# Expert products' scratch laid out by token tile and second half-key, two expert blocks stored at once

## What is computed

```
def _peer(x, wq, keys, u_tab, v_tab):
    ...
    s = jnp.einsum('thcd,hcnd->thcn', q, keys)
    v1, i1 = lax.top_k(s[:, :, 0], PEER_TOPK)
    v2, i2 = lax.top_k(s[:, :, 1], PEER_TOPK)
    ...
    cidx = (i1[..., :, None] * N_KEYS + i2[..., None, :])...
    top_s, pos = lax.top_k(cand, PEER_TOPK)
    ...
        a = jnp.einsum('td,tkd->tk', xt, u_tab[it])
        hid = (gelu(a) * gt)
        return jnp.einsum('tk,tkd->td', hid, v_tab[it])
```

## Time and profile before

| | us |
|---|---|
| median of 3 runs | 3742.63 (3737.31 to 3744.31) |
| the profiled execution, its own time | 3735.37 |
| its span | 3733.6 |
| PE busy | 2471.0 (66%) |
| DVE busy | 2762.9 (74%) |
| POOL busy | 1246.5 (33%) |
| ACT busy | 332.7 (9%) |

### The profile page before, as it was taken

The page is one execution under the profiler, slowest core; times in us unless marked ns, Lnnn a source line. Parts: engine busy times, 40 slices in busy tenths (PEclk is TensorE's granted clock), DMA queues, the critical chain, the costliest instruction groups (busy, mean ns, idle before and its releaser), DMA issues.

```text
span 3733.6 us, 30440 instructions
## 1 busy us (share of the span) xinstructions
PE 2471.0 (66%) x11208; PEld 1892.2 (51%) x11208; DVE 2762.9 (74%) x3210; ACT 332.7 (9%) x832; POOL 1246.5 (33%) x1273
## 2 busy tenths in 40 slices
PE   7798799978975777959988999999978000000000
PEld 7687689545743444535677877777767000000000
DVE  5331220979989997787789889976655999988888
ACT  1212311000002221000100000000000000000000
POOL 2420000122233332223222223232222577777772
PEclk9899899988986657989999999999999555555555
DMA  8774355898998999989999999999998999999998
GB/s 245 219 232 121 143 190 179 292 397 332 341 405 343 406 419 375 422 343 414 421 422 423 423 423 423 423 421 424 423 382 336 413 407 410 409 390 370 392 373 348
DMA packets 297908, 1332.43 MB, mean 357 GB/s; under 512 B 70752, under 2 KB 136832, under 8 KB 146336
## 3 DMA queue, kind: packets, MB, share of 16 engines
q0 software_dynamic: 138624, 945.22, 62.9%
q1 hardware_dynamic: 126400, 371.83, 26.7%
q10 hardware_dynamic: 32736, 13.44, 1.4%
HBM read 1282.60 MB, written 57.20 MB: 359 GB/s over the span
## 4 chain that ended last, share of the span: by engine, by line
PE 35%; DMA 27%; DVE 22%; POOL 8%; issue 6%; another core or an unknown queue 1%; ACT 1%; ACTq 1%; SPq 0%; DVEq 0%; POOLq 0%
PE low L1559 18%; DMA arena<-in_ut 16%; PE low L1900 10%; DVE arena L1375 7%; DVE acc L1391 5%; DMA arena<-in_peer_v,arena 5%; POOL arena L611 4%; POOL arena L620 4%; DMA arena<-in_w 2%; DMA arena<-in_peer_u,arena 2%; PE low L1633 1%; PE acc L1633 1%; DMA arena<-y_scratch_b 1%; DVE low L1391 1%
## 5 line engine op out<-in xcount | busy, mean ns | idle before, releaser
L1391 DVE SCALAR_TENSOR_TENSOR acc<-arena,acc 128x2048 f32<-128x2048 f32 x443 | 1042.6, 2354 | 262.4 <-DMA arena<-in_peer_v,arena 226.7
L1559 PE MATMUL low<-arena 128*128 128x192 f32 (+1 forms) x4096 | 1064.8, 420 | 100.6 <-DMA arena<-in_w 77.3
L1900 PE MATMUL low<-arena 128*128 128x256 f32 x4096 | 915.5, 383 | 110.1 <-DMA arena<-in_ut 109.0
L1559 PEld LDWEIGHTS low<-arena 128*128 128x128 f32 x4096 | 738.3, 196 | 376.0 <-DMA arena<-in_w 74.6
L1900 PEld LDWEIGHTS low<-arena 128*128 128x128 f32 x4096 | 774.1, 191 | 251.3 <-DMA arena<-in_ut 133.2
L611 POOL DMA_INDIRECT arena<-in_peer_v,arena x576 | 579.5, 1006 | 924.3 <-DVE acc L1391 772.6
L1375 DVE SCALAR_TENSOR_TENSOR arena<-arena,acc 128x2048 f32<-128x2048 f32 x320 | 724.8, 2284 | 115.3 <-DMA arena<-in_peer_u,arena 107.6
L611 POOL DMA_INDIRECT arena<-in_peer_u,arena x320 | 320.1, 1000 | 1185.6 <-DVE arena L1375 856.1
L1391 DVE SCALAR_TENSOR_TENSOR low<-arena,low 128x2048 f32<-128x2048 f32 x126 | 296.6, 2354 | 35.8 <-DMA arena<-in_peer_v,arena 26.8
L620 POOL DMA_INDIRECT arena<-expert_scratch,arena x256 | 263.3, 1029 | 83.2 <-issue 83.2
L872 ACT COPY arena<-low 128x256 f32<-128x256 f32 x128 | 47.6, 372 | 971.0 <-PE low L1900 957.9
(11 more groups left out here) (274 smaller groups left out, 1678.3 us busy)
## 6 DMA issues: line engine op xcount, KB each, us to landing
arena<-in_w SPq DMA_DIRECT2D x128, 1024.0 KB
arena<-in_ut SPq DMA_DIRECT2D x128, 1024.0 KB
expert_scratch<-arena SPq DMA_DIRECT2D x128, 128.0 KB
arena<-in_peer_v,arena POOLq DMA_INDIRECT x576
arena<-toeplitz_scratch SPq DMA_DIRECT2D x64, 128.0 KB, 3.6
arena<-c_scratch SPq DMA_DIRECT2D x64, 128.0 KB, 4.2
bias_scratch<-distance_scratch SPq DMA_DIRECT2D x1, 5120.0 KB, 23.4
x_scratch<-arena ACTq DMA_DIRECT2D x5, 1024.0 KB
```

The source lines that it names most:

```text
L1391: stt(held, slot[j], wv_, held, ALU.mult, ALU.add).then_inc(used, 1)
L1559: ins = mm(L[n % 2][:, 0:width], wring[n % 2][:, k, :], rhs(k), start=k == 0, stop=k == KT - 1)
L1900: ins = mm(L[j % 4][:, 0:NSD], ud[j % 4][:, k, :], lane(catB, k)[:, P:NB], start=k == 0, stop=k == KT - 1)
```

## The change

The staging is two buffers of two blocks each, in place of four of one. A pair's buffer holds, per partition (one i2), first the 128 tokens of tile 3 for both blocks and then those of tile 4. ACT's copy writes its block's part as two runs of 128 elements. SP stores once for two blocks, at every second j (odd, from 5), blocks j-5 and j-4. In HBM the array is now ordered (tile, i2, i1, token) and was (i1, i2, tile, token); its size is the same. The pick addresses follow: (128 * i2 + i1) * 128 + token, plus 2097152 for tile 4, in place of (128 * i1 + i2) * 256 + token, plus 128 for tile 4.

```
-        astg = [at(H2 + D + NSD * j, NSD) for j in range(4)]
+        astg = [at(H2 + D + 2 * NSD * j, 2 * NSD).rearrange("p (u n) -> p u n", u=2) for j in range(2)]
...
-        ascr = nc.dram_tensor("expert_scratch", [EB * P * NSD, 1], F32).ap()
+        ascr = nc.dram_tensor("expert_scratch", [2 * P * EB * P, 1], F32).ap()
...
-            def products_out(j):
-                sp.wait_ge(a_out, j + 1)
-                sp.dma_start(ascr.rearrange("(j p t) o -> j p (t o)", p=P, t=NSD)[j], astg[j % 4]
-                             ).then_inc(a_st[j % 4], 16)
+            def products_out(b):
+
+                sp.wait_ge(a_out, 2 * b + 2)
+                sp.dma_start(ascr.rearrange("(u p b n) o -> b p u (n o)", u=2, p=P, n=2 * P)[b], astg[b % 2]
+                             ).then_inc(a_st[b % 2], 16)
...
-                if j >= 4:
-                    products_out(j - 4)
+                if j >= 5 and j % 2:
+                    products_out((j - 5) // 2)
...
-            for j in range(EB - 4, EB):
-                products_out(j)
+            for b in range(EB // 2 - 2, EB // 2):
+                products_out(b)
...
-            for b in range(4):
+            for b in range(2):
                 pool.wait_ge(a_st[b], 16 * EB // 4)
...
-                    if j >= 4:
-                        act.wait_ge(a_st[j % 4], 16 * (j // 4))
-                    nc.scalar.copy(astg[j % 4], L[j % 4][:, 0:NSD]).then_inc(a_out, 1)
+                    if j >= 4 and j % 2 == 0:
+                        act.wait_ge(a_st[j // 2 % 2], 16 * (j // 4))
+                    nc.scalar.copy(astg[j // 2 % 2].rearrange("p u (i t) -> p i u t", i=2)[:, j % 2],
+                                   L[j % 4][:, 0:NSD].rearrange("p (u t) -> p u t", u=2)).then_inc(a_out, 1)
...
-                    link(stt(flat, row[0], float(NKEY), row[1], ALU.mult, ALU.add))
-                    link(ts_(idxe[:, KK * (t - NGU):KK * (t - NGU) + KK], flat, float(NSD),
+                    link(stt(flat, row[1], float(NKEY), row[0], ALU.mult, ALU.add))
+                    link(ts_(idxe[:, KK * (t - NGU):KK * (t - NGU) + KK], flat, float(P),
...
-        "tok_off": np.stack([np.arange(P), np.arange(P) + P], axis=1).astype(np.float32),
+        "tok_off": np.stack([np.arange(P), np.arange(P) + P * EB * P], axis=1).astype(np.float32),
```

More of the change, by code:

```diff
@@ L352, in build @@
         ud_used, a_out = sem("ud_used"), sem("a_out")
-        a_st = [sem(f"a_stored{j}") for j in range(4)]
+        a_st = [sem(f"a_stored{j}") for j in range(2)]
         ln2_in, early_in, late_in = sem("ln2_in"), sem("early_sums_in"), sem("late_x1_in")
```

## The result

The changed kernel takes 3717.57 us (median of 4 runs, 3716.53 to 3718.16) against 3740.49 for the kernel before (4 runs beside it); the ratio is 0.9938 with a 95% interval of 0.9921 to 0.9955. So it is faster by 23 us, where no change was forecast and the range began at 3720. The profiled execution has a span of 3714.6 us, 19.0 less than before.

A forecast was written before the change was run, and what follows sets the result against it. DMA engine time, by packets in the loop, was taken as the bound. The span 3733.6 - 0.6 + 0 = 3733 us, plus 1.8 and 7.3 us to the median of runs, gave 3742; range 3720 to 3768.

The forecast's parts named there:

- What bounds the kernel: Block loop: the DMA engines take both queues' packets nearly one for one; 7.85 us a block computed, 7.96 seen.
- Stores, bytes and packets: Stores in the loop: 16384 packets of 1 KB stay; 64 fewer stores save 0.6 us; the rest taken as 0.
- The prediction's own sign: In the loop: the prediction is wrong if q1's share (37.5%) or the packet count moves.
- the wide step: Stores: neighbouring partitions' runs lie 64 KB apart in HBM; taken as 0; rival of slower writes 3791 us, chance 0.12.
- Loop's end: DVE's 24.68 us wait for ACT's copy of block 125 and layer norm instruction: change 0, at worst 1 us.
- The third rival: A store comes out as 128 packets of 2 KB, not 256; PE at 7.17 us a block; 3718 us, chance 0.04.
- Order in SP's queue: Two loads, then a double store: PE's two small gaps become one, same sum, 15.7 us a pair; costs nothing.
- ACT's wait: Every second ACT copy waits about 3.5 us for a store, one at the early loads about 34; covered, cost 0.
- Picks: 256 gathers of 128 single products at the end, as before: 0, bounded by -25 and +27 us.
- gone stretch: Rival at the end of the kernel: the picks' slow stretch disappears; 3717 us, chance 0.15.
- slow stretch: Picks from 3300 to 3640 us: 379 GB/s against 409 at nearly the same mix, unexplained by the trace.

## Why the prediction was wrong

*What bounds the kernel.* Right, and the key lay in it: "the engines take them nearly one for one, whatever their size". The rule held wherever both queues were filled. Its account of a block was short by the completion packets, though: 128 + 128 + 32 packets of q1 pass, and about 288 of q0, of which 256 are rows. (A slip beside it: the stores carry one byte in 25 of the loop, not in 26.)

*Stores, bytes and packets.* Here it failed. "64 stores fewer save 64 completion packets per engine, 64 x 0.01 = 0.6 us" prices the packet at its own time and forgets the turn, which had just been found. Half a turn a block, at 8/9 of the 0.311 us of a row packet, is 0.14 us; over the 102 blocks from copy 13 to copy 115 that is 14 us, and these took 14.4 us less (793.8 us before, 779.4 after). The whole loop got 13.9 us shorter. The term was too small by a factor of more than 20. The prediction's own sign, q1's share or count moving, showed it: 37.5% to 38.1%, and 15029 to 14789 packets. The rest of this part held: 1 KB runs, 16 x 64 = 1024 packets fewer in all, and the wide step is free, as the old layout's equal time shows. Of the power-of-two pitches in the Trainium skill (DMA: Bandwidth & Descriptors, Latency and other measured facts), 64 KiB thus behaves like its 512 KiB row and not like its 4 MiB one, at least for these writes of 1 KB beside another queue (loop 988.7 against 989.1 us).

*Loop's end.* "0, at worst 1 us" took DVE's 24.68 us as fixed. It was the only place where a quicker loop could be turned into time. In the runs the wait fell to 0.4 us, and the traffic of those 70 us rose by what 15.3 us of the engines carry. The third rival had this mechanism and its price right (3718 for a shift of turns), but was tied to packets of 2 KB and given 0.04; that its number came true is in part luck, since no such packets came. Had the completion packets been counted as turns there, it would have been the forecast.

*Order in SP's queue.* Right but for the length of the pair (15.7 us forecast, 15.28 measured). PE has one gap a pair, of 1.06 us (1.3 forecast), at a clock of 1.00:

```profile
2411.84 14.08 PE L1902 MATMUL low<-arena 128*128 128x256 f32 x64 [1.06 <-DMA arena<-in_ut]
```

*ACT's wait.* Right in size and in being covered:

```profile
2406.95 0.37 ACT L873 COPY arena<-low 128x256 f32<-128x256 f32 x1 [10.88 <-DMA expert_scratch<-arena]
```

The bracket holds all of ACT's idle time and puts it down to what ended it. PE had begun this pair at 2396.71, so the bank was ready at 2403.8, and the wait for the store is 3.2 us (3.5 forecast). At the early loads PE finished block 116 at 2771.98 us and ACT copied it at 2800.32, a wait of 28 us (34 forecast):

```profile
2800.32 0.37 ACT L873 COPY arena<-low 128x256 f32<-128x256 f32 x1 [39.30 <-DMA expert_scratch<-arena]
```

PE never waited for ACT in the loop; its 88.8 us of idle time there all end with a load.

*Picks.* The rival "gone stretch" would have given nearly the measured time for a wrong reason. From 3300 to 3640 us it is 388 GB/s in place of 379, so the slow stretch is still there, if less slow. The prediction named a change of these figures as a sign of being wrong; the 5 us that lie in it are the part that stays open.

## What to carry to other kernels

When two DMA queues are both full as here, count packets, not bytes: each packet of one, a completion packet among them, lets a packet of the other pass, and costs that one's time. Fewer and longer packets on a queue give it a larger share, and thereby take it from the other. Such a shift was worth only the idle time that it removed at the next meeting point of the two streams, so find that point first; moving the waiting instruction there may give most of the same.

## What the runs showed of the hardware

A completion packet, or a data packet of 4 bytes, on the queue of SP cost 0.26 to 0.32 us beside a full queue of 8 KB packets, and one of 512 B 0.28; beside a nearly empty one they cost nothing that was seen. The Trainium skill (DMA: Bandwidth & Descriptors, Queues, rings and completion order) tells of turns too, but of a whole group of some 9 to 17 descriptors a turn. The equal counts here, 12139 to 12139 with data packets of 512 B and 8 KB, are turns of one packet as the profile records it. Equal counts alone would not tell the two apart in the kernel before, where a load, a store and a gather all bring nine packets to an engine. With runs of 512 B a store brings 17: taken in whole groups, q1 would have had 26 packets for 18 of q0.
